# Rows transposed before their normalisation, and the multiplications that keep TensorE occupied at two starts

## The chip, the cores and the metric

The kernel runs on one core of a Trainium2 chip. The metric is the device time of one execution in microseconds (us). TensorE multiplies, VectorE, ScalarE and GpSimd do the elementwise work, and SyncE issues most of the DMAs. The rows of the profile call them PE (PEld is its weight load), DVE, ACT, POOL and SP.

## What is computed

Two layers of a decoder trunk for 512 prompt rows and 64 sample rows, 1024 wide, in f32. The change touches the first step of each layer, the normalisation and the input product, and the gating half `u` that comes out of it:

```python
def rmsnorm(x, g):
    y = x * rsqrt(mean(x * x, axis=-1) + EPS)
    return y * g

z = rmsnorm(x, g1) @ w_in                 # 1024 x 2560
a = gelu(z[..., :2 * D_A])                # u | va, 512 columns each
u, va = a[..., :D_A], rmsnorm(a[..., D_A:], av_g)
q, k = rmsnorm over heads of 64 columns;  vb = the last 512 columns
x = x + concat(u * chunk_mix(va), diff_attention(q, k, vb)) @ w_out
x = x + hierarchical_moe(rmsnorm(x, g2))  # 16 experts, two per row
```

The root `rsqrt(mean(x*x)+EPS)` is one number per row of x, so it can be multiplied onto x before the product or onto z after it.

## The kernel before

The rows stand in five tiles of 128 rows (`NT` = 5), four of the prompt and a fifth (`TP` = 4) with the 64 sample rows. One program holds every engine's instructions in an order that is written by hand; the engines meet in semaphores. `full[u]` says that PE has filled the PSUM bank `u`, `read[u]` that it has been read; `claim(u)` is PE's wait for the latter. The banks of this document are S0 and S1 (products of rows), T0 and T1 (transposes), J, I, O, and F (products of the gates). `keep_busy` multiplies the identity with itself into a bank that nobody reads.

**The input product.** For each tile ACT squares the row and sums it (`square_first`, L1150), POOL makes the root from the sum (`rsqrt`, L515 and L517), DVE multiplies x by the root into `hn` (`scaled`, L1387), PE transposes `hn` in two halves of four blocks (`turn_rows`, L671), and DVE multiplies the transpose by the gain g1 into `hT` (`turned`, L1393). PE then multiplies `hT` with the weights, which lie in a ring of six pieces of 1 MB; two pieces make 512 columns of w_in. The columns come in the order k, v, q, u, va. The transposes of tile t+1 are issued in the k columns of tile t, behind six of its eight steps (`rows`). ACT evacuates the products (`evacuate`) and squares those of k and q for the head norms.

**The gates.** `large("u", j)` computes u transposed, with the weights stationary, into the bank F; ACT applies Gelu from F into `catT`. u0 and u1 stand around the transposes of k, u2, u3 and the sample's `us` stand in the steps 0, 1 and 2 of the attention loop (`LARGE`). In a step n, PE does the scores of head n, transposes the probabilities of head n-2 (`turn_probs`), then the large product of the step and the small works of the sample (`ss` is the sample's scores, also in F), and multiplies the probabilities of head n-3 with v. DVE finds the maxima (`biggest`) and combines the two softmaxes (`combine`).

**The layer boundary.** The experts' results are scattered into `y_rows` by POOL and loaded back by ACT (`high_load`); DVE adds them to x (`add_high`, L1867), which releases `x_ready`. Then the chain of the input product begins again for layer 1. PE's own end of layer 0 is one multiplication of `flush`. SP issues the DMAs of the start in the order x tile 0, the identity (`id_in`), g1, weight pieces 0 and 1, x tiles 1 to 3 and the sample's, constants, pieces 2 to 5.

A matmul in f32 shows as two rows of the trace: eight steps of 128x512 are sixteen rows.

## Time and profile before

| | us |
|---|---|
| median of 3 runs | 1022.43 |
| lowest and highest | 1020.42, 1023.01 |
| the profiled execution | 1022.66 |
| its span, first to last instruction | 1020.8 |
| PE busy in it | 962.5 (94%) |
| mean granted clock of PE | 0.982 |

The span is the time from the first to the last instruction; the profiled execution is 1.86 us longer than it. PE is busy for 94% of the span, so an engine's work matters where PE waits for it. A granted clock of 1.00 is 2.4 GHz and one of 0.50 is 1.2 GHz.

### The profile page before, as it was taken

How to read it: one execution, taken by the hardware profiler on the slowest of the kernel's cores; microseconds unless marked ns; L12 is line 12 of the kernel's file. 1: busy time of each engine (PE TensorE's matmuls, PEld its weight loads, DVE VectorE, ACT ScalarE, POOL GpSimd, SP SyncE). 2: the span in 40 equal slices, each digit the busy share in tenths (PEclk: the TensorE clock that was granted, in tenths of full speed). 3: DMA queues.
4: the chain of work that ended last, by engine and by line, in shares of the span. 5: the costliest groups of instructions: out<-in, count | busy, mean ns of one | idle time of the engine just before them, and what ended most of it. 6: DMA issues, size and time to landing. Idle time of an engine off the chain costs nothing.

```text
span 1020.8 us, 13578 instructions
## 1 busy us (share of the span) xinstructions
PE 962.5 (94%) x4918; PEld 495.4 (49%) x4918; DVE 440.4 (43%) x1154; ACT 233.3 (23%) x483; POOL 191.5 (19%) x265
## 2 busy tenths in 40 slices
PE   6999999999998999999599999999989989999991
PEld 4444455556456444434254344655555554444340
DVE  2403122566346466551343111345563565555523
ACT  2101255542001011111121114555220011111110
POOL 2333201331101111111125031022220011111100
PEclk9999999999998999999899999999999999999996
DMA  8716003342511979998742150134252059799946
GB/s 335 267 31 257 1 1 129 103 146 91 220 42 63 383 259 370 420 421 328 240 144 83 49 209 1 68 109 160 63 208 103 21 222 367 274 381 412 403 153 209
DMA packets 39769, 197.72 MB, mean 194 GB/s; under 512 B 7632, under 2 KB 7760, under 8 KB 23824
## 3 DMA queue, kind: packets, MB, share of 16 engines
q1 hardware_dynamic: 19744, 136.22, 34.0%
q0 software_dynamic: 15888, 45.87, 12.8%
q10 hardware_dynamic: 4064, 14.68, 4.0%
q8 instruction: 42, 0.69, 0.3%
q14 instruction: 31, 0.25, 0.1%
HBM read 177.35 MB, written 29.88 MB: 203 GB/s over the span
## 4 chain that ended last, share of the span: by engine, by line
PE 84%; DVE 6%; DMA 4%; issue 2%; POOL 1%; ACT 1%; POOLq 0%; SPq 0%; ACTq 0%; DVEq 0%
PE ps L673 77%; PE ps L671 6%; DMA cat<-y_rows 1%; DMA x<-in_xp 1%; POOL st L517 1%; PE ps L688 1%; DMA y_rows<-hn,isca 1%; DVE cat L1720 1%; DVE hT L1393 0%; DMA hT<-h_rows,igat 0%; DVE tmp L1542 0%; DVE st L1543 0%; ACT hn L1306 0%; DVE st L1510 0%; DVE o_sb L1530 0%
## 5 line engine op out<-in xcount | busy, mean ns | idle before, releaser
L673 PE MATMUL ps<-ring,hT 128*128 128x512 f32 (+2 forms) x1056 | 382.4, 595 | 2.9 <-DVE hT L1393 2.5
L673 PEld LDWEIGHTS ps<-ring,hT 128*128 128x128 f32 (+2 forms) x1056 | 148.9, 166 | 198.1 <-issue 196.9
L673 PE MATMUL ps<-ring,cat 128*128 128x512 f32 (+2 forms) x560 | 195.4, 596 | 2.6 <-ACT hn L1306 2.4
L673 PEld LDWEIGHTS ps<-ring,cat 128*128 128x128 f32 (+2 forms) x560 | 72.9, 162 | 82.3 <-issue 79.4
L617 POOL DMA_INDIRECT y_rows<-hn,isca x28 | 28.1, 1003 | 250.1 <-ACT hn L1306 219.5
L673 PE MATMUL ps<-hT,ring 128*128 128x512 f32 (+1 forms) x256 | 71.8, 437 | 0.3 <-ACT cat L1194 0.3
L515 POOL TENSOR_SCALAR st<-st 128x1 f32<-128x1 f32 (+3 forms) x60 | 16.3, 272 | 282.2 <-ACT sqj L1150 106.4
L517 POOL TENSOR_TENSOR st<-st,half 128x1 f32<-128x1 f32 (+3 forms) x60 | 62.5, 1042 | 11.6 <-POOL st L515 11.1
L1861 DVE TENSOR_TENSOR hT<-ps,par 128x512 f32<-128x512 f32 x56 | 36.0, 685 | 56.0 <-PE ps L671 55.6
L1414 DVE TENSOR_REDUCE st<-sqj 128x8 f32<-128x512 f32 x20 | 13.5, 681 | 108.3 <-ACT sqj L1165 108.2
L1306 ACT COPY hn<-ps 128x1024 f32<-128x1024 f32 x28 | 28.4, 1013 | 118.3 <-PE ps L673 118.3
L673 PEld LDWEIGHTS ps<-hT,ring 128*128 128x128 f32 x256 | 38.1, 191 | 29.6 <-issue 28.4
L523 POOL DMA_DIRECT2D kc<-in_ck x32 | 25.3, 791 | 99.8 <-PE ps L673 78.8
L688 PE MATMUL ps<-c 128*128 128x128 f32 x164 | 27.4, 333 | 15.5 <-DVE x L1867 9.8
L1510 DVE TENSOR_REDUCE st<-ps 128x2 f32<-128x256 f32 (+3 forms) x32 | 26.3, 821 | 36.4 <-PE ps L673 36.3
L1231 ACT ACTIVATE ring<-ps,st 128x128 f32<-128x128 f32 (+3 forms) x64 | 33.2, 524 | 38.3 <-DVE st L1511 38.2
L610 POOL DMA_INDIRECT hT<-h_rows,igat x28 | 28.7, 1025 | 59.6 <-DVE isca L1759 30.3
L1165 ACT ACTIVATE sqj<-ps 128x512 f32<-128x512 f32 (+1 forms) x20 | 11.9, 596 | 119.1 <-PE ps L673 119.1
L1755 DVE TENSOR_REDUCE o_sb<-ps 128x4 f32<-128x12 f32 (+2 forms) x18 | 3.0, 167 | 83.5 <-PE ps L673 83.5
L1150 ACT ACTIVATE sqj<-x 128x1024 f32<-128x1024 f32 x10 | 10.6, 1058 | 121.1 <-DVE x L1576 100.6
L673 PE MATMUL ps<-vc,hT 128*128 128x512 f32 (+2 forms) x112 | 36.5, 598 | 0.8 <-issue 0.8
L523 POOL DMA_DIRECT2D vc<-in_cv x32 | 17.7, 552 | 91.4 <-PE ps L673 76.1
(249 smaller groups left out, 1172.7 us busy)
## 6 DMA issues: line engine op xcount, KB each, us to landing
ring<-in_w SPq DMA_DIRECT2D x82, 1024.0 KB
kc<-in_w SPq DMA_DIRECT2D x12, 1024.0 KB
vc<-in_w SPq DMA_DIRECT2D x10, 1024.0 KB
v<-in_w SPq DMA_DIRECT2D x10, 1024.0 KB
kva<-in_w SPq DMA_DIRECT2D x10, 1024.0 KB
kc<-in_ck POOLq DMA_DIRECT2D x32, 256.0 KB, 3.6
vc<-in_cv POOLq DMA_DIRECT2D x32, 256.0 KB, 3.2
h_rows<-qk ACTq DMA_DIRECT2D x10, 512.0 KB, 2.6
```

What stands on the lines that cost most here:

```text
L515: nc.gpsimd.tensor_scalar(stat["ms"][at, 0:n], src, 1.0 / size, EPS, ALU.mult, ALU.add).then_inc(*pool_c.inc())
L517: nc.gpsimd.tensor_tensor(dst, stat["ms"][at, 0:n], half[at, 0:n], ALU.pow).then_inc(*pool_c.inc(*label))
L523: pool.dma_start(buffer(b % 2, g), view(d[table][bass.DynSlice(l * NPOOL + page, 1)])).then_inc(*arrived[b % 2].inc("kv", b, by=16))
L610: pool.indirect_dma_start(hs[:, b, :], None, h_rows, bass.IndirectOffsetOnAxis(index, 0), bounds_check=TOK - 1, oob_is_err=False).then_inc ...
L617: pool.indirect_dma_start(rows, bass.IndirectOffsetOnAxis(index, 0), y_sb[:, b, :], None, bounds_check=rows.shape[0] - 1, oob_is_err=False ...
L671: ins = pe.transpose(out, lhsT, rhs)
L673: ins = pe.matmul(out, lhsT, rhs, start=start, stop=stop, skip_group_check=loose)
L688: pe.matmul(bank("J")[:, 0:P], ident, ident)
L1231: ins = nc.scalar.activation(e_sb[:, n % 2, m, 0:(i + 1) * P], bank(f"S{n % 2}", m)[:, 0:(i + 1) * P], ACT.Exp, bias=stat["nb"][:, c:c + 1 ...
L1306: nc.scalar.copy(y_sb[:, b, :], ps[:, 6:8, :].rearrange("p a n -> p (a n)")).then_inc(*read["O"].inc("down", *key))
L1510: link(vec.tensor_reduce(stat["mx"][:, c:c + 2], ps[:, b0:b0 + 2, 0:(i + 1) * P], AX.X, ALU.max))
L1861: vec.tensor_tensor(hsT[:, b, hf * HALF:(hf + 1) * HALF, :], bank(f"T{hf}").rearrange("p (j t) -> p j t", j=HALF), g, ALU.mult).then_inc(* ...
```

## The change

- **Transposes of x itself.** `scaled` is gone from the input product of both layers. PE transposes x as soon as the tile is there: in layer 0 when its load has landed, in layer 1 when `add_high` has released `x_ready`.
- **The root on the products.** ACT's evacuations of k, v, q and va multiply by the root of the row with the instruction's scale. u is transposed, so its roots must lie along the free axis: `root_diagonals` (DVE) multiplies the identity by each tile's roots, PE multiplies these by a matrix of ones behind the k columns (five matmuls into T0 and T1), and DVE copies the result into `roots`. `scale_gates` (DVE) multiplies each u product by them into `tmp`; Gelu (ACT) then reads `tmp`. The bank F is now released by DVE for u.
- **Places.** At the layer boundary DVE no longer waits two tiles behind `add_high`; `turned(t-1)` follows `add_high(t)` directly. One `memset` of hn is split, its second half stands in step 3 of the attention loop. ACT's Gelu of u0 and u1 moved behind the copies of kT and of qT.
- **Multiplications into nowhere.** At the start 18 multiplications of the 64-column tile `half` with itself, as soon as POOL has written it, in place of 12 with the identity when it has landed. At the boundary 30 of the identity into I right behind layer 0's last product, in place of 10 into J behind `x_ready`.

```diff
-            def keep_busy(n):
-                claim("J")
+            def keep_busy(n, u="J", operand=ident):
+                claim(u)
+                cols = operand.shape[-1]
                 for _ in range(n):
-                    pe.matmul(bank("J")[:, 0:P], ident, ident)
+                    pe.matmul(bank(u)[0:cols, 0:cols], operand, operand)
...
+            pe.wait_ge(*pool_c.at("half"))
+            keep_busy(18, operand=half[:, :])
             pe.wait_ge(id_in.sem, 16)
-            keep_busy(12)
             for l in layers():
                 if l:
-                    pe.wait_ge(x_ready.sem, l * NT + 1)
-                    keep_busy(10)
+                    keep_busy(30, "I")
+                def turn_input(t):
+                    if l == 0:
+                        pe.wait_ge(*dve_s.at("blank"))
+                        pe.wait_ge(x_in[t].sem, 16)
+                    turn_rows("h1", t, (x_ready.sem, l * NT + (t + 1)))
...
                 rows("k", 0)
+                pe.wait_ge(*dve_s.at("diagonals"))
+                for t in range(NT):
+                    u, n = ("T0", P) if t < TP else ("T1", NROW)
+                    if t in (0, TP):
+                        claim(u)
+                    mm(bank(u)[:, t % TP * P:t % TP * P + n], ones, diagonals[:, t * P:t * P + n], inc=full[u].inc("roots") if t >= TP - 1 else None)
                 rows("v", 1)
...
                         act.wait_ge(*full[u].at("z", name, t))
+                        act.wait_ge(*pool_c.at("rs1", t))
                         if name in "kq":
                             square_heads(name, t, u, slice(0, P))
-                        nc.scalar.copy(dst[:, t, :], bank(u)).then_inc(*read[u].inc("z", name, t))
+                        nc.scalar.mul(dst[:, t, :], bank(u), stat["rs"][:, t:t + 1]).then_inc(*read[u].inc("z", name, t))
...
                     if name == "u":
-                        nc.scalar.activation(catT[:, j, 0:TP * P], bank("F"), ACT.Gelu_apprx_tanh).then_inc(*read["F"].inc(name, j))
+                        act.wait_ge(*read["F"].at(name, j))
+                        nc.scalar.activation(catT[:, j, 0:TP * P], tmp[:, :], ACT.Gelu_apprx_tanh).then_inc(*act_s.inc(name, j))
...
+                def root_diagonals():
+                    vec.memset(ones, 1.0)
+                    for t in range(NT):
+                        dve.wait_ge(*pool_c.at("rs1", t))
+                        ins = vec.tensor_scalar(diagonals[:, t * P:(t + 1) * P], ident, stat["rs"][:, t:t + 1], None, ALU.mult)
+                    ins.then_inc(*dve_s.inc("diagonals"))
...
                     for t in range(NT):
                         if t == NT - 1:
                             sums("k", 0)
-                        scaled(t)
                         turned(t)
                     sums("k", 1)
+                    root_diagonals()
                     constants()
+                else:
+                    root_diagonals()
...
+                def scale_gates(name, j):
+                    dve.wait_ge(*full["F"].at(name, j))
...
+                    if before:
+                        dve.wait_ge(*act_s.at(*before))
+                    vec.tensor_tensor(out, src, by, ALU.mult).then_inc(*read["F"].inc(name, j))
+
+                for j in range(2):
+                    scale_gates("u", j)
                 dve.wait_ge(*read[HEADS_IN[TP]].at("qT", TP))
...
+                        elif name != "va":
+                            scale_gates(name, j)
+                    if n == 3:
+                        dve.wait_ge(*act_s.at("us", 0))
+                        link(vec.memset(hn[:, 1, :], 0.0))
...
-                for t in range(NT + 4):
-                    if 2 <= t < NT + 2:
-                        add_high(t - 2)
+                for t in range(NT + 1):
+                    if t < NT:
+                        add_high(t)
                     if l + 1 < L:
                         Count.layer = l + 1
-                        if 3 <= t < NT + 3:
-                            scaled(t - 3)
-                        if t == NT + 3:
+                        if t == NT:
                             sums("k", 0)
-                        if t >= 4:
-                            turned(t - 4)
-                        if t == NT + 3:
+                        if t >= 1:
+                            turned(t - 1)
+                        if t == NT:
                             sums("k", 1)
```

The lines moved with the edit: the changed kernel's L673 is L671 of before (transposes), L675 is L673 (products), L691 is L688 (`keep_busy`), L1412 is L1393 (`turned`) and L1918 is L1867 (`add_high`).

PE at the start of the program, before (x12 is twelve of them in a row; `c` holds the identity):

```order
L688 MATMUL ps<-c 128x128 x12
L671 MATMUL ps<-c,hn 128x128 x8
L673 MATMUL ps<-ring,hT 128x512 x6
L671 MATMUL ps<-c,hn 128x128 x8
L673 MATMUL ps<-ring,hT 128x512 x8
L671 MATMUL ps<-c,hn 128x128 x8
L673 MATMUL ps<-ring,hT 128x512 x8
L671 MATMUL ps<-c,hn 128x128 x8
L673 MATMUL ps<-ring,hT 128x512 x8
L671 MATMUL ps<-c,hn 128x128 x8
L673 MATMUL ps<-ring,hT 128x512 x34
L673 MATMUL ps<-ring,hT 64x512 x16
```

and of the changed kernel:

```order
L691 MATMUL ps<-half 64x64 x18
L673 MATMUL ps<-c,x 128x128 x8
L675 MATMUL ps<-ring,hT 128x512 x6
L673 MATMUL ps<-c,x 128x128 x8
L675 MATMUL ps<-ring,hT 128x512 x8
L673 MATMUL ps<-c,x 128x128 x8
L675 MATMUL ps<-ring,hT 128x512 x8
L673 MATMUL ps<-c,x 128x128 x8
L675 MATMUL ps<-ring,hT 128x512 x8
L673 MATMUL ps<-c,x 128x128 x8
L675 MATMUL ps<-ring,hT 128x512 x2
L675 MATMUL ps<-hn 128x128 x4
```

The small multiplications stand ahead of the transposes, these read x, and five matmuls of `hn` (the diagonals) stand between k and v.

PE at the boundary of the layers, before:

```order
L149 UNCONDITIONAL_BRANCH
L152 UNCONDITIONAL_BRANCH
L688 MATMUL ps<-c 128x128 x10
L671 MATMUL ps<-c,hn 128x128 x8
L673 MATMUL ps<-ring,hT 128x512 x6
L671 MATMUL ps<-c,hn 128x128 x8
L673 MATMUL ps<-ring,hT 128x512 x8
```

and of the changed kernel:

```order
L149 UNCONDITIONAL_BRANCH
L152 UNCONDITIONAL_BRANCH
L691 MATMUL ps<-c 128x128 x30
L673 MATMUL ps<-c,x 128x128 x8
L675 MATMUL ps<-ring,hT 128x512 x6
L673 MATMUL ps<-c,x 128x128 x8
L675 MATMUL ps<-ring,hT 128x512 x8
```

The 30 multiplications are in the place of the 10, but no longer behind the wait for `x_ready`, and the diagonals stand here too.

DVE at the boundary, before (L1867 is `add_high` where it reads `cat`, L1387 is `scaled`, L1393 is `turned`):

```order
L1867 SCALAR_TENSOR_TENSOR x<-cat,st,x 128x1024 x2
L1387 TENSOR_SCALAR hn<-x,st 128x1024
L1867 SCALAR_TENSOR_TENSOR x<-cat,st,x 128x1024
L1387 TENSOR_SCALAR hn<-x,st 128x1024
L1393 TENSOR_TENSOR hT<-ps,g_sb 128x4x128 x2
L1867 SCALAR_TENSOR_TENSOR x<-cat,st,x 128x1024
L1387 TENSOR_SCALAR hn<-x,st 128x1024
L1393 TENSOR_TENSOR hT<-ps,g_sb 128x4x128 x2
L1867 SCALAR_TENSOR_TENSOR x<-cat,st,x 64x1024
L1387 TENSOR_SCALAR hn<-x,st 128x1024
L1393 TENSOR_TENSOR hT<-ps,g_sb 128x4x128 x2
L1387 TENSOR_SCALAR hn<-x,st 128x1024
```

and of the changed kernel:

```order
L1918 SCALAR_TENSOR_TENSOR x<-cat,st,x 128x1024 x2
L1412 TENSOR_TENSOR hT<-ps,g_sb 128x4x128 x2
L1918 SCALAR_TENSOR_TENSOR x<-cat,st,x 128x1024
L1412 TENSOR_TENSOR hT<-ps,g_sb 128x4x128 x2
L1918 SCALAR_TENSOR_TENSOR x<-cat,st,x 128x1024
L1412 TENSOR_TENSOR hT<-ps,g_sb 128x4x128 x2
L1918 SCALAR_TENSOR_TENSOR x<-cat,st,x 64x1024
L1412 TENSOR_TENSOR hT<-ps,g_sb 128x4x128 x2
L1433 TENSOR_REDUCE st<-sqj 128x8
L1412 TENSOR_TENSOR hT<-ps,g_sb 128x4x128 x2
L1433 TENSOR_REDUCE st<-sqj 128x8
L1436 MEMSET hn 128x128
```

`turned` of tile 0 moved up from behind three `add_high` and two `scaled` to behind two `add_high`, and the matrix of ones with the diagonals stands at the end.

## Rows read from the trace of the kernel before

**Rows 1.** Section 4 of the page: shares of the chain that ended last.

```profile
PE 84%; DVE 6%; DMA 4%; issue 2%; POOL 1%; ACT 1%; POOLq 0%; SPq 0%; ACTq 0%; DVEq 0%
```

**Rows 2.** Timeline of the start: start us, us, engine, line, work [idle before <-releaser].

```profile
5.53 1.06 ACT L1150 ACTIVATE o_sb<-x 128x1024 f32<-128x1024 f32 x1 [3.07 <-DMA x<-in_xp]
...
5.73 4.39 PE L688 MATMUL ps<-c 128*128 128x128 f32 x24 [5.73 <-DMA c<-in_c]
...
9.24 0.75 DVE L1387 TENSOR_SCALAR hn<-x,st 128x1024 f32<-128x1024 f32 x1 [5.50 <-DMA g_sb<-in_g]
...
10.74 1.29 DVE L1393 TENSOR_TENSOR hT<-ps,g_sb 128x512 f32<-128x512 f32 x2 [0.75 <-PE ps L671]
...
12.29 5.39 PE L673 MATMUL ps<-ring,hT 128*128 128x512 f32 x12 [1.15 <-DVE hT L1393]
...
15.36 1.06 ACT L1150 ACTIVATE o_sb<-x 128x1024 f32<-128x1024 f32 x1 [8.68 <-DMA x<-in_xp]
...
18.65 1.09 PE L671 MATMUL ps<-c,hn 128*128 128x128 f32 x8 [0.98 <-DVE hn L1387]
```

**Rows 3.** Busy time by stretch of the start; (x) counts instructions.

```profile
core 0: us, PE busy (x) PEld busy (x) DVE busy (x) ACT busy (x) POOL busy (x), PEclk, DMA share, GB/s
7.00:8.00 1.00, 1.00 (x6) 1.00 (x6) 0.00 (x0) 0.00 (x0) 0.74 (x2) 1.00 0.90 318
9.00:10.00 1.00, 1.00 (x11) 0.93 (x9) 0.75 (x1) 0.00 (x0) 0.00 (x0) 1.00 1.04 426
10.00:14.00 4.00, 2.85 (x14) 1.72 (x13) 1.29 (x2) 0.00 (x0) 0.00 (x0) 1.00 1.00 417
```

**Rows 4.** Timeline of the boundary between the layers.

```profile
498.08 0.27 PE L671 MATMUL ps<-c 128*128 128x128 f32 x1
...
506.79 1.28 DVE L1867 SCALAR_TENSOR_TENSOR x<-cat,st,x 128x1024 f32<-128x1024 f32 x1 [6.99 <-DMA cat<-y_rows]
...
508.13 4.63 PE L688 MATMUL ps<-c 128*128 128x128 f32 x20 [9.78 <-DVE x L1867]
...
508.80 1.28 DVE L1867 SCALAR_TENSOR_TENSOR x<-cat,st,x 128x1024 f32<-128x1024 f32 x1 [0.73 <-DMA cat<-y_rows]
...
514.14 1.28 DVE L1393 TENSOR_TENSOR hT<-ps,g_sb 128x512 f32<-128x512 f32 x2
...
515.68 5.39 PE L673 MATMUL ps<-ring,hT 128*128 128x512 f32 x12 [1.39 <-DVE hT L1393]
```

**Rows 5.** Busy time and granted clock of two microseconds at the boundary.

```profile
503.00:504.00 1.00, 0.00 (x0) 0.00 (x0) 0.00 (x0) 0.00 (x0) 0.00 (x0) 0.87 0.00 0
513.00:514.00 1.00, 1.00 (x6) 1.00 (x6) 0.53 (x1) 0.97 (x2) 0.36 (x1) 0.51 0.85 269
```

**Rows 6.** The same ahead of the experts, in layer 0 and in layer 1.

```profile
315.00:316.00 1.00, 0.33 (x3) 0.33 (x4) 1.00 (x3) 0.41 (x2) 0.30 (x1) 1.00 0.88 360
316.00:317.00 1.00, 1.00 (x7) 1.00 (x6) 0.28 (x2) 0.10 (x1) 0.68 (x2) 0.50 0.41 164
817.00:818.00 1.00, 0.22 (x3) 0.16 (x2) 0.92 (x3) 0.58 (x2) 0.13 (x1) 1.00 0.72 291
```

**Rows 7.** Timeline of the end of the k columns of layer 0.

```profile
42.57 1.29 DVE L1393 TENSOR_TENSOR hT<-ps,g_sb 128x512 f32<-128x512 f32 x2 [5.20 <-PE ps L671]
...
43.78 0.68 DVE L1414 TENSOR_REDUCE st<-sqj 128x8 f32<-128x512 f32 x1
...
44.73 0.60 ACT L1165 ACTIVATE sqj<-ps 128x512 f32<-128x512 f32 x1 [6.67 <-PE ps L673]
...
46.89 0.48 DVE L1433 TENSOR_TENSOR tmp<-par 128x64 f32<-128x64 f32 x2
```

**Rows 8.** Timeline of the attention loop's steps 3 and 4, layer 0.

```profile
159.01 0.58 ACT L1247 ACTIVATE ring<-ps,st 128x384 f32<-128x384 f32 x1
...
159.25 0.33 PE L671 MATMUL ps<-c,ring 128*128 128x128 f32 x1
...
159.73 7.13 PE L673 MATMUL ps<-ring,hT 128*128 128x512 f32 x16 [0.15 <-ACT ring L1247]
```

More of the change, by code:

```diff
@@ L262, in program @@
                   v[:, 0:TP, :].rearrange("p t n -> p (t n)"), kva[:, 0:TP, :].rearrange("p t n -> p (t n)")]
+        diagonals = hn[:, 0, 0:NT * P]
+        roots, ones = hn[:, 1, 0:TOK], hn[:, 1, TOK:TOK + P]
         rows_of = sb("rows_of", [P, NT, E, 4], BF16)
@@ L502, in _ @@
         def _(pool):
-            nc.gpsimd.memset(half[:, :], -0.5).then_inc(*pool_c.inc())
+            nc.gpsimd.memset(half[:, :], -0.5).then_inc(*pool_c.inc("half"))
             pool.dma_start(pages[:, :], d["pages"]).then_inc(*pages_in.inc(by=16))
@@ L724, in rows @@
                             if t == 0:
-                                turn_rows("h1", 0, dve_s.at("hn1", 0))
+                                turn_input(0)
                             claim(u)
@@ L735, in rows @@
                             if c == 0 and k == KD - 3:
[L736 removed]
+                                turn_input(t + 1)
                 def sample_rows(name, low, high):
@@ L1164, in square_heads @@
                         act.wait_ge(*dve_s.at("ssk", NT - 1))
-                    nc.scalar.activation(sqj[at, t % 2, :], bank(u)[at, :], ACT.Square).then_inc(*act_s.inc("sq", name, t))
+                    nc.scalar.activation(sqj[at, t % 2, :], bank(u)[at, :], ACT.Square, scale=stat["rs"][at, t:t + 1]).then_inc(*act_s.inc("sq", name, t))
                 def evacuate(name, dst):
@@ L1185, in _ @@
                 square_heads("q", TP, "S0", LOW)
-                nc.scalar.copy(qz[LOW, TP, :], bank("S0")[LOW, :])
-                nc.scalar.activation(kva[HIGH, TP, :], bank("S0")[HIGH, :], ACT.Gelu_apprx_tanh).then_inc(*read["S0"].inc("z", "qva"))
+                nc.scalar.mul(qz[LOW, TP, :], bank("S0")[LOW, :], stat["rs"][LOW, TP:TP + 1])
+                nc.scalar.activation(kva[HIGH, TP, :], bank("S0")[HIGH, :], ACT.Gelu_apprx_tanh, scale=stat["rs"][HIGH, TP:TP + 1]).then_inc(*read["S0"].inc("z", "qva"))
                 act.wait_ge(*read["S0"].at("z", "qva"))
@@ L1202, in large @@
                         act.wait_ge(*dve_s.at("ssq", NT - 1))
-                    nc.scalar.activation(kva[:, j, :], bank("F"), ACT.Gelu_apprx_tanh).then_inc(*read["F"].inc(name, j))
+                    nc.scalar.activation(kva[:, j, :], bank("F"), ACT.Gelu_apprx_tanh, scale=stat["rs"][:, j:j + 1]).then_inc(*read["F"].inc(name, j))
                     act.wait_ge(*read["F"].at(name, j))
@@ L1434, in _ @@
                 vec.tensor_reduce(stat["lam"][:, 0:2], groups(tmp[:, 0:2 * DK], 2, DK), AX.X, ALU.add).then_inc(*dve_s.inc("lamdot"))
-                link(vec.memset(hn[:, :, :], 0.0))
+                dve.wait_ge(*full["T0"].at("roots"))
+                vec.tensor_copy(roots[:, 0:TP * P], bank("T0")).then_inc(*read["T0"].inc("roots"))
+                dve.wait_ge(*full["T1"].at("roots"))
+                vec.tensor_copy(roots[:, TP * P:TP * P + NROW], bank("T1")[:, 0:NROW]).then_inc(*read["T1"].inc("roots"))
+                link(vec.memset(hn[:, 0, :], 0.0))
                 for t in range(2, NT):
```

29 lines of the change are left out of this document (18 added, 11 removed).

## The prediction

> **What bounds the kernel now.** I read the page's chain of waits first: the reader is to see that PE holds 84% of it [rows 1], so a microsecond counts only where PE waits or does more. There are two places where PE waits for the input of a layer, and the change works on both; I then read their timelines, and last the places where the change puts new work beside PE.
>
> The start [rows 2]: x tile 0 has landed at 5.53, the identity at 5.73. PE multiplies the identity until DVE has made hn. DVE could not start that before 9.24, when g1 landed. The transposes are evacuated from 10.74, and 0.26 behind the end of that, at 12.29, PE starts its first product. It does 12 rows of it, then waits for the transposes of tile 1, which begin at 18.65: that tile landed at 15.36, and the square, root and multiplication took the 3.29 between. From 18.65 on the chain is PE without a gap.
>
> The boundary [rows 4]: PE's last row starts at 498.08 and ends at 498.35. It is idle until add_high of tile 0 is through at 508.07, and the first product starts at 515.68, again 0.26 behind the end of turned (514.14 + 1.28).
>
> The clock: at the boundary it fell from 2.4 to 1.2 GHz about 5.4 after PE's last row (granted 0.87 in the microsecond from 503), and rose 5.8 after PE had begun again (0.51 in that from 513) [rows 5]. At the start the record says 1.00 throughout, but the rows say otherwise: 6 of the 128x128 instructions in the microsecond from 7, 11 in that from 9 [rows 3].
>
> **The change, part by part,** against the profiled execution, 1022.66 (span 1020.8 and 1.86 around it, 0.23 above the median).
>
> *Start.* turned(0) needs g1 (9.24) and no longer hn: 9.24 + 1.29 + 0.26 = 10.79 is the earliest that PE can begin [rows 2]. The weights may be later. Tile 1, 0.52 MB, landed at 15.34 behind pieces 0 and 1 of 1.05 MB; at the 417 GB/s of 10 to 14 [rows 3] this puts piece 1 at 15.34 - 1.25 = 14.1 and piece 0 at 14.1 - 2.5 = 11.6, if they land in the order of issue; before, both were in time for 12.29. I take 11.3. The 12 rows last 12 x 0.43 = 5.15, so tile 1's transposes begin at 16.5 and not at 18.65: -2.2, between -2.7 (10.79) and -1.4 (12.0). The tile's landing (15.36) is hidden under that product. ACT's square and POOL's root are not removed, but they are now wanted only by the evacuation, 7 later.
>
> *Boundary.* DVE does add_high(0), add_high(1), turned(0). The second add waits for its data and ends at 508.80 + 1.28 = 510.08 [rows 4]; PE's transposes (508.1 to 509.8 even at 1.2 GHz) are ready by then. So turned ends at 510.08 + 1.28 = 511.36 and PE begins at 511.6 in place of 515.68: -4.0, between -4.1 and -3.5 if a semaphore or a later add comes between. Tile 1's transposes are wanted some 5 later and its add is done. Nothing else on DVE's or SP's queue is late: pieces 2 and 3 are wanted only at the v columns, 26 later.
>
> *Roots as a row.* PE does five more matmuls, ten rows, at 128 columns. In the fast microsecond eleven such rows start [rows 3], so this is 10 x 0.107 = 1.07 a layer. PE also waits for the diagonals. In layer 0 the k columns end at 44.73 (ACT's square of the last tile) and DVE's sum ends at 43.78 + 0.68 = 44.46 [rows 7]. Behind it now come a memset and five small multiplications. The nearest row is a 128x64 product, two in 0.48 [rows 7]: five at 0.15 to 0.3 and the memset 0.15 give 0.9 to 1.65; I take 1.15, near that row's 0.24 less the overlap that two without a wait between have. That ends at 45.6, plus a semaphore's 0.1: PE waits 1.0, between 0.7 and 1.5. Both ends move together with tile 4's transposes, so the start's gain does not cover it. Layer 1 has the same order. Sum: 2 x 2.07 = +4.1, between +3.5 and +5.1. Behind it, the copies of the roots and the split memset lie under v's 27 of PE.
>
> *Scaled evacuations.* A copy of 128x512 becomes an ACTIVATE; ACT's own, with a scale or without, take 0.60 [rows 7], there are 6.9 for each, and the roots are long there: nothing. If a root were late, PE would wait at the next claim of S0 or S1.
>
> *Gates through DVE.* The change adds a wait on DVE: in steps 0 to 2 scale_gates stands ahead of combine and biggest, so these, and ACT's exponentials behind them, wait for the product. PE spends these times in the next product (7.1), which hides them. What is visible is bank F: DVE needs 0.69 where ACT needed 0.60, three times 0.1 at most. In step 3 the chain us, Gelu, table, probabilities, sample's exponential (159.01) releases F for the first va product, for which PE waited 0.15 [rows 8]; with one more engine in it I add 0.4. The transposes of q gain 0.2, since ACT has no Gelu ahead of them. +0.3 a layer, together +0.6, between -0.4 and +1.2.
>
> Sum without the clock: -2.2 - 4.0 + 4.1 + 0.6 = -1.5, 1021.1 (between -3.9 and +1.3).
>
> *The clock.* The transposes now come early and the product late. At the start PE's small multiplications end near 5 (36 rows of half the columns, each half as long as a slow one of [rows 3], 3 to 4 in all, begun in the second microsecond), the transposes near 7, and the product starts at 11.3: some 4.5 idle. At the boundary 60 rows at 0.107 end at 504.9 if they start at once, at 506.5 if PE's branches take what they may; then idle to 508.1, 0.9 of transposes, and 2.6 idle until 511.6. Before, 5.4 of idling cost the clock [rows 5]. Ahead of the experts less was enough in layer 0: PE was a third busy in the microsecond from 315 and the clock read 0.50 from 316; in layer 1 a like stretch (0.22 busy from 817) kept it [rows 6]. So the new gaps are near the edge, and a second stretch of low activity in a row speaks for the fall. What a fall costs: the work done at half rate after the restart lasted 3 at the start (rows of 5.73 to about 8.8) and 5.8 at the boundary; half of it is lost, 1.5 to 2.9. I take 1.5 at the start and 2.3 at the boundary, where the fall may come late.
>
> The Trainium skill's page "TensorE: Matmul & The Clock Gate", section "What's actually happening", says that half rate is the default and activity releases it. By that rule alone the changed kernel pays at both places and ends at 1024.9; without a fall it ends at 1021.1. The rows at the boundary agree with the rule; those ahead of the experts show that the edge isn't sharp.
>
> **The rivals.**
> 1. *Both products start at 1.2 GHz* (forecast): -1.5 + 1.5 + 2.3 = +2.3, 1024.9. Chance 0.42.
> 2. *One of the two does*: -1.5 + 1.9 = +0.4, 1023.0. For it: layer 1 ahead of the experts kept its clock. 0.33.
> 3. *Neither*: 1021.1. The new multiplications carry the clock over. Against it are the 4.5 and the 2.6 of idling. 0.12.
> 4. *DVE becomes late in the attention loop*, the slower side. PE's transposes of head 2 stand at 159.25 [rows 8]; the combine ahead of them now starts behind the scaling of us, 156.2 + 0.4, and ends near 157.5. It decides from 1.8 of further lateness on (the memset of hn and the wait for Gelu stand right there); then F and the probabilities are late together, about 2 a layer: 1024.9 + 4 = 1028.9. 0.06.
> 5. *The start and the roots are better than priced*: piece 0 is there at 10.8, the diagonals cost 0.7 and both clocks hold: -3.9 or a little below, 1018.5. 0.07.
>
> That the change does not do what it says can only be at the start: if piece 0 lands at 12, the early transposes bring 1.4 and not 2.2; it is in the bounds.
>
> **How the numbers follow.** Beside these the half-rate stretch ahead of the experts may come or go with the shift, 1 to 1.5 either way. The range of eight in ten goes from a little below case 3, 1020.0, to 1028.0, which takes in case 1 with dear clocks (2.9 twice) and the roots at 5.1. About 0.3% (3.1) is what a measurement of this kernel can tell. Slower than 1025.5: four tenths of case 1, case 4, a little of 2: 0.27. Faster than 1019.4: case 5, a third of 3, some of 2: 0.16. The same: 0.57.
>
> **What would show it.** In the changed trace: the first 128x512 row near 11.3 and at 511.6; the distance of such rows, 0.43 at 2.4 GHz or 0.85 at 1.2 GHz, over the first dozen of each; a wait of PE of 1.0 for DVE ahead of ten rows that read hn, near 42 and 543; and the first va product, 0.4 later against the scores of step 3. The forecast is wrong if those rows stand 0.43 apart from the first, or if the wait for the diagonals is gone, because then the balance falls to the faster side.

## The result and the profile after

| | before | changed |
|---|---|---|
| median (22 runs each), us | 1020.5 | 1022.6 |
| lowest and highest | 1017.29, 1023.01 | 1020.95, 1025.15 |
| the profiled execution | 1022.66 | 1021.79 |
| its span | 1020.8 | 1020.1 |
| PE's last row ends | 998.74 | 999.74 |

The ratio is 1.0021 [1.0013, 1.0029]: the change costs 2.1 us. The forecast was +2.3 against the profiled execution, which gave 1024.9, and "the same" as the likeliest of faster, same and slower; the time lies inside the stated range, but the interval of the ratio leaves no room for "the same". The profiled execution of before lay 2.2 above the median of the 22 runs, and most of the difference between 1024.9 and 1022.6 comes from that.

The profiled executions alone say the opposite, 0.9 faster for the changed kernel. One pair can't be trusted at this size. At PE's end the changed kernel is 1.0 behind; then the chain goes through the last load of `y_rows` (start, duration, what), before:

```profile
1005.31 9.06 DMA cat<-y_rows
```

and in the changed kernel:

```profile
1006.34 7.48 DMA cat<-y_rows
```

No instruction of the change stands there. The page of the changed kernel, busy time, granted clock by slice and the chain:

```profile
PE 970.8 (95%) x4990; PEld 502.1 (49%) x4990; DVE 442.4 (43%) x1172; ACT 239.4 (23%) x485; POOL 191.4 (19%) x265
...
PEclk9999999999999999999989999999999999999996
...
PE 86%; DVE 6%; DMA 3%; issue 2%; ACT 1%; POOL 1%; SPq 0%; ACTq 0%; DVEq 0%; POOLq 0%
```

PE holds 86% of the chain where it held 84% [rows 1]: it waits less and does more.

**The start.** Timeline of the changed kernel, which answers to [rows 2]:

```profile
1.21 4.07 PE L691 MATMUL ps<-half 128*64 128x64 f32 x36 [1.21 <-POOL half L505]
...
5.66 1.51 PE L673 MATMUL ps<-c,x 128*128 128x128 f32 x8 [0.39 <-DMA c<-in_c]
...
7.76 1.29 DVE L1412 TENSOR_TENSOR hT<-ps,g_sb 128x512 f32<-128x512 f32 x2 [4.03 <-DMA g_sb<-in_g]
...
10.42 6.86 PE L675 MATMUL ps<-ring,hT 128*128 128x512 f32 x12 [3.25 <-DMA ring<-in_w]
...
12.26 0.34 PEld L675 LDWEIGHTS ps<-ring,hT 128*128 128x128 f32 x1 [0.52 <-issue]
13.11 0.33 PEld L675 LDWEIGHTS ps<-ring,hT 128*128 128x128 f32 x1 [0.52 <-issue]
...
14.04 1.06 ACT L1165 ACTIVATE o_sb<-x 128x1024 f32<-128x1024 f32 x1 [7.43 <-DMA x<-in_xp]
14.12 0.19 PEld L675 LDWEIGHTS ps<-ring,hT 128*128 128x128 f32 x1 [0.24 <-issue]
14.54 0.19 PEld L675 LDWEIGHTS ps<-ring,hT 128*128 128x128 f32 x1 [0.24 <-issue]
...
17.12 1.04 PE L673 MATMUL ps<-c,x 128*128 128x128 f32 x8
```

g1 landed at 7.76 and not at 9.24, the input was ready at 9.05, and PE then waited for weight piece 0 until 10.42. Twelve rows lasted 6.86 where they had lasted 5.39 [rows 2]: their weight loads stand 0.85 apart at 12.26 and 13.11, and 0.42 apart at 14.12 and 14.54. Tile 1 had landed by 14.04, well under the product. Tile 1's transposes begin at 17.12, 1.53 sooner than before; without the loss of 1.5 to the clock it would be 3.0.

**The boundary.** The same view of the boundary, which answers to [rows 4]:

```profile
497.78 0.27 PE L673 MATMUL ps<-c 128*128 128x128 f32 x1
...
499.36 6.94 PE L691 MATMUL ps<-c 128*128 128x128 f32 x60 [1.31 <-issue]
...
507.75 2.55 DVE L1918 SCALAR_TENSOR_TENSOR x<-cat,st,x 128x1024 f32<-128x1024 f32 x2 [8.30 <-DMA cat<-y_rows]
...
509.09 1.97 PE L673 MATMUL ps<-c,x 128*128 128x128 f32 x8 [2.80 <-DVE x L1918]
...
510.24 0.69 DVE L1412 TENSOR_TENSOR hT<-ps,g_sb 128x512 f32<-128x512 f32 x1
...
511.09 0.69 DVE L1412 TENSOR_TENSOR hT<-ps,g_sb 128x512 f32<-128x512 f32 x1 [0.16 <-PE ps L673]
...
512.05 6.93 PE L675 MATMUL ps<-ring,hT 128*128 128x512 f32 x12 [0.99 <-DVE hT L1412]
...
518.81 1.04 PE L673 MATMUL ps<-c,x 128*128 128x128 f32 x8
```

From the end of PE's last row (498.05; 498.35 before) to the first product it is now 14.00 and was 17.33: 3.33 less. The twelve rows last 6.93 and not 5.39, so tile 1's transposes are only 1.79 sooner by the same measure. add_high(0) could start 9.70 behind PE's last row and not 8.44 behind it as before [rows 4]; from its start to the product it is 4.30, and was 8.89.

The granted clock of the changed kernel at both places, in microseconds from 9, 10, 508 and 515 (columns as in [rows 3]):

```profile
9.00:10.00 1.00, 0.00 (x0) 0.00 (x0) 0.05 (x1) 0.00 (x0) 0.00 (x0) 0.99 1.00 418
10.00:11.00 1.00, 0.58 (x1) 0.50 (x2) 0.00 (x0) 0.00 (x0) 0.00 (x0) 0.50 1.03 434
...
508.00:509.00 1.00, 0.00 (x0) 0.00 (x0) 1.00 (x1) 0.00 (x0) 0.00 (x0) 0.66 0.99 401
515.00:516.00 1.00, 1.00 (x3) 0.46 (x3) 0.00 (x0) 0.00 (x0) 1.00 (x2) 0.92 0.77 172
```

At the start the record has 2.4 GHz until 10, in the idle time behind the transposes, and 1.2 GHz when the product begins. At the boundary it falls earlier, in the 2.8 of idling between the 30 multiplications and the transposes, so these run at half rate as well. Before, both products ran at 2.4 GHz (5.39 for twelve rows [rows 2, rows 4]), with the multiplications of the identity right ahead of the transposes; e4 and e6 put these back, one place each, and the product there takes 5.39 again.

**The roots.** The end of layer 0's k columns in the changed kernel, which answers to [rows 7]:

```profile
42.19 0.68 DVE L1433 TENSOR_REDUCE st<-sqj 128x8 f32<-128x512 f32 x1
42.84 0.17 DVE L1436 MEMSET hn<- 128x128 f32 x1
42.92 1.07 DVE L1439 TENSOR_SCALAR hn<-c,st 128x128 f32<-128x128 f32 x5
...
44.05 1.33 PE L675 MATMUL ps<-hn 128*128 128x128 f32 x10 [0.95 <-DVE hn L1439]
...
45.21 5.37 PE L675 MATMUL ps<-ring,hT 128*128 128x512 f32 x12
```

PE waits 0.95 for the diagonals (0.81 in layer 1) and spends 1.16 on ten rows.

**The gates.** The first va product of layer 0, which answers to [rows 8], starts its rows behind a wait of 0.41, where it was 0.15:

```profile
160.74 0.70 PE L675 MATMUL ps<-ring,hT 128*128 128x512 f32 x1 [0.41 <-ACT ring L1268]
```

Laid along PE's own path, the two profiles give this table. A stretch runs from one landmark to the next; the last row but one holds the router and the experts, which the change doesn't touch.

| stretch of PE (us) | before | changed | difference |
|---|---|---|---|
| start to tile 1's transposes | 18.65 | 17.12 | -1.53 |
| from there to u0, layer 0 and 1 | 95.14, 95.08 | 97.41, 97.28 | +2.27, +2.20 |
| u0 to the output product, layer 0 and 1 | 97.57, 97.55 | 97.81, 97.95 | +0.24, +0.40 |
| last row of layer 0 to tile 1's transposes of layer 1 | 22.55 | 20.76 | -1.79 |
| output product to the layer's last row, layer 0 and 1 | 286.99, 285.21 | 285.71, 285.70 | -1.28, +0.49 |
| behind PE's last row | 22.06 | 20.36 | -1.70 |

The change's own rows add up to -1.53 + 4.47 + 0.64 - 1.79 = +1.8, and the medians give +2.1. The two last rows are the noise in which these stand: the half-rate stretch ahead of the experts ran from 316.0 to 322.8 before [rows 6] and from 317.4 to 320.3 after, and in layer 1 there is one only in the changed kernel.

The first row holds such a chance too. In e10, whose start is that of the kernel before, tile 1 had landed by 14.05 and not 15.36, and its transposes began at 17.42 and not at 18.65. So 1.2 of the 1.53 come from a late load in one execution of before; against e10's start the sum would be +3.0, so that +1.8 and +2.1 lie so close is in part luck.

### The profile page after: what moved, and what is told of

It is laid out like the page before. It is cut to its first block, busy times and chain, and to the rows that moved or that the text cites. A ratio compares the mean times of both kernels' runs of the same rounds, so it can differ in the third digit from the quotient of the medians.

```text
span 1020.1 us, 13761 instructions
## 1 busy us (share of the span) xinstructions
PE 970.8 (95%) x4990; PEld 502.1 (49%) x4990; DVE 442.4 (43%) x1172; ACT 239.4 (23%) x485; POOL 191.4 (19%) x265
## 4 chain that ended last, share of the span: by engine, by line
PE 86%; DVE 6%; DMA 3%; issue 2%; ACT 1%; POOL 1%; SPq 0%; ACTq 0%; DVEq 0%; POOLq 0%
PE ps L675 78%; PE ps L673 7%; PE ps L691 1%; DMA cat<-y_rows 1%; POOL st L519 1%; DMA y_rows<-hn,isca 1%; DMA ring<-in_w 1%; DVE cat L1771 1%; DVE hT L1412 1%; DVE tmp L1588 0%; DVE st L1589 0%; ACT hn L1327 0%; DVE st L1556 0%; DVE o_sb L1576 0%; DVE tmp L1547 0%
## 5 line engine op out<-in xcount | busy, mean ns | idle before, releaser
L675 PE MATMUL ps<-ring,hT 128*128 128x512 f32 (+2 forms) x1056 | 385.8, 598 | 5.1 <-DMA ring<-in_w 3.2
L675 PEld LDWEIGHTS ps<-ring,hT 128*128 128x128 f32 (+2 forms) x1056 | 150.3, 168 | 201.0 <-issue 199.3
L675 PE MATMUL ps<-ring,cat 128*128 128x512 f32 (+2 forms) x560 | 195.4, 597 | 2.6 <-ACT hn L1327 2.4
L675 PEld LDWEIGHTS ps<-ring,cat 128*128 128x128 f32 (+2 forms) x560 | 73.0, 163 | 82.2 <-issue 79.3
L675 PE MATMUL ps<-hT,ring 128*128 128x512 f32 (+1 forms) x256 | 71.8, 438 | 0.5 <-DVE tmp L1498 0.5
L519 POOL TENSOR_TENSOR st<-st,half 128x1 f32<-128x1 f32 (+3 forms) x60 | 62.9, 1048 | 11.6 <-POOL st L517 11.4
L675 PEld LDWEIGHTS ps<-hT,ring 128*128 128x128 f32 x256 | 38.2, 191 | 29.9 <-issue 28.4
L1180 ACT ACTIVATE sqj<-ps,st 128x512 f32<-128x512 f32 (+1 forms) x20 | 13.7, 686 | 100.5 <-PE ps L675 94.0
L675 PE MATMUL ps<-vc,hT 128*128 128x512 f32 (+2 forms) x112 | 36.5, 598 | 0.8 <-issue 0.8
L1412 DVE TENSOR_TENSOR hT<-ps,g_sb 128x512 f32<-128x512 f32 x20 | 13.0, 687 | 54.5 <-PE ps L673 50.5
L1316 ACT ACTIVATE cat<-ps 128x256 f32<-128x256 f32 x28 | 10.7, 383 | 95.2 <-PE ps L675 95.2
```

The source lines that it names most:

```text
L519: nc.gpsimd.tensor_tensor(dst, stat["ms"][at, 0:n], half[at, 0:n], ALU.pow).then_inc(*pool_c.inc(*label))
L675: ins = pe.matmul(out, lhsT, rhs, start=start, stop=stop, skip_group_check=loose)
L1180: nc.scalar.activation(sqj[at, t % 2, :], bank(u)[at, :], ACT.Square, scale=stat["rs"][at, t:t + 1]).then_inc(*act_s.inc("sq", name, t))
L1412: vec.tensor_tensor(hT[:, hf * HALF:(hf + 1) * HALF, t * P:(t + 1) * P], bank(f"T{hf}").rearrange("p (j t) -> p j t", j=HALF), g, ALU.mult ...
```

## The experiments

Every ratio is to the kernel before, measured on the same chip beside it; the changed kernel stands at 1.0021. Each edit is on the changed kernel, except that of e10.

**e1: the gaps filled.** Multiplications of the identity behind tile 0's transposes too, and 42 in place of 30 at the boundary.

```diff
-                    keep_busy(30, "I")
+                    keep_busy(42, "I")
...
                             if t == 0:
                                 turn_input(0)
+                                keep_busy(8 if l else 14)
```

> The changed kernel with PE occupied in its gaps: 14 multiplications of the identity between the transposes of tile 0 and the first product of layer 0, 8 there in layer 1, and 42 in place of 30 at the boundary. Theory (the half-rate clock costs 1.7 at the start and 1.5 to 1.8 at the boundary): the granted clock stays at 1.00 over both, the first twelve rows of 128x512 take 5.2 in place of 6.9 at each, and the kernel is 3.3 faster than the changed one, about 1.3 faster than before (ratio 0.9987). Rival (the fillers themselves come late and push the product, or the weights and DVE bound it anyway): the first products begin 1 to 3 later and the time is within 0.5 of the changed kernel's 1.0021.

Measured: 1021.56, 1.0007 [0.9994, 1.0021]. Timeline of PE at the start and the boundary:

```profile
6.64 3.29 PE L691 MATMUL ps<-c 128*128 128x128 f32 x28
10.39 5.39 PE L675 MATMUL ps<-ring,hT 128*128 128x512 f32 x12 [0.47 <-DMA ring<-in_w]
...
497.69 9.62 PE L691 MATMUL ps<-c 128*128 128x128 f32 x84 [2.06 <-issue]
507.14 1.04 PE L673 MATMUL ps<-c,x 128*128 128x128 f32 x8
508.02 1.95 PE L691 MATMUL ps<-c 128*128 128x128 f32 x16
509.80 5.32 PE L675 MATMUL ps<-ring,hT 128*128 128x512 f32 x12
```

Both products run at full rate (5.39 and 5.32 for twelve rows), the boundary's transposes take 1.04 and not 1.97, and tile 1's transposes start at 15.62, 1.50 sooner than in the changed kernel. So the loss at the two products is the clock's, and the idle time ahead of them is what brings it. e1 fills both gaps of the boundary in one edit, the one ahead of the transposes and the one behind them. The other profiles show that the fall can come in either: with the boundary's program unchanged, the clock fell ahead of the transposes in the changed kernel and e8 (transposes 1.97), and behind them in e2, e3 and e6 (transposes 1.09, granted 0.50 or 0.62 in the microsecond from 512, 515 and 513). But the ratios show 1.4 and not 3 or more, and their intervals overlap. The profiled execution took 1018.28 at a mean granted clock of 0.992; the others lie between 0.985 and 0.990, and the six at 0.985 or 0.986 took 1021.6 to 1023.0. Something else loses the clock in them: e9 looks at that.

**e2: u left unscaled.** The five matmuls, the diagonals and the copies are gone and `roots` is filled with ones; u is left without its roots. This changes the values that reach the router, and the whole time (1049.85, 1.0284) can't be used: in its profile 50.62 lie behind PE's last row, where the changed kernel has 20.36. The stretch up to u0 can be used.

```diff
-                pe.wait_ge(*dve_s.at("diagonals"))
-                for t in range(NT):
...
-                    mm(bank(u)[:, t % TP * P:t % TP * P + n], ones, diagonals[:, t * P:t * P + n], inc=full[u].inc("roots") if t >= TP - 1 else None)
...
+                vec.memset(roots[:, 0:TP * P + NROW], 1.0)
```

> The changed kernel without the row of roots: no diagonals, no five matmuls and no wait for them; the gates are multiplied by ones, so u is left unscaled. It prices that part alone. Theory (0.9 to 1.0 of waiting and 1.1 to 1.2 of matmuls in each layer, all on the path): PE goes from the k to the v columns without a gap and the time is 4.1 less than the changed kernel's, ratio 0.998 against before. Rival (part of it is hidden or given back later, and the loss sits in the gates' way through DVE): 2 less or under, ratio 1.000.

Measured, from tile 1's transposes to u0: 95.08 in both layers, where the changed kernel has 97.41 and 97.28. The row of roots costs 2.33 + 2.20 = 4.5. In PE's timeline k runs into v in one group:

```profile
41.28 19.05 PE L675 MATMUL ps<-ring,hT 128*128 128x512 f32 x44
```

**e3: the roots one tile later.** The same five matmuls, behind the first tile of the v columns in place of behind k.

```diff
-                pe.wait_ge(*dve_s.at("diagonals"))
-                for t in range(NT):
...
+                            if (c, t, k) == (1, 0, KD - 1):
+                                row_of_roots()
```

> The changed kernel with the five matmuls of the roots behind the first tile of the v columns, 6.9 later. Theory (of the 2.1 a layer 0.9 is the wait for DVE's diagonals): that wait is gone, the matmuls' 1.1 stays, 1.8 less than the changed kernel in all, ratio 1.0004. Rival (the wait moves to another place, since DVE's copies of the roots and the sums behind them are now later): no gain, ratio 1.002.

Measured: 1020.5, 1.0006 [0.9991, 1.0021]; from tile 1's transposes to u0 96.20 in both layers, which is 1.2 and 1.1 less than in the changed kernel and 1.1 more than without roots. The ratio's interval overlaps that of the changed kernel, so the step is shown by the stretch, not by the whole time. PE's timeline has no wait at them:

```profile
45.80 6.17 PE L675 MATMUL ps<-ring,hT 128*128 128x512 f32 x14
51.81 1.22 PE L675 MATMUL ps<-hn 128*128 128x128 f32 x10
```

Of the 2.2 a layer one half is the wait, which is only a matter of place; the other half is the ten rows themselves.

**e4: the old boundary.** 10 multiplications into J behind `x_ready`, all else as changed.

```diff
-                    keep_busy(30, "I")
+                    pe.wait_ge(x_ready.sem, l * NT + 1)
+                    keep_busy(10)
```

> The changed kernel with the boundary's multiplications as before: ten of the identity behind x_ready, into bank J, everything else as changed. Theory: the transposes of tile 0 now end about 4.7 behind x_ready at half rate, so the product begins about 2.5 later than in the changed kernel, but with the clock risen or about to rise it gets 1 to 1.5 back: 1 to 1.5 slower than the changed kernel (ratio 1.0033). Rival (what counts at the boundary is that the clock has risen when the product begins, not when the product begins): equal to or faster than the changed kernel, ratio 1.002 or less.

Measured: 1023.39, 1.0042 [1.0029, 1.0055]. The profile of e4:

```profile
508.17 4.64 PE L691 MATMUL ps<-c 128*128 128x128 f32 x20 [10.16 <-DVE x L1919]
512.60 1.09 PE L673 MATMUL ps<-c,x 128*128 128x128 f32 x8
515.00 5.39 PE L675 MATMUL ps<-ring,hT 128*128 128x512 f32 x12 [1.31 <-DVE hT L1413]
```

With transposes of x but twenty slow rows ahead of them, the product starts 16.99 behind the last row (498.01), against 14.00 in the changed kernel and 17.33 before: nearly the whole gain of the boundary comes from the moved multiplications, since the transposes were waiting for them and not for `scaled`. The product then runs at full rate, so the net of the move is 1.5 in the profile (tile 1's transposes 22.2 behind the last row, 20.8 in the changed kernel), and 0.21% by the ratios.

**e6: the old start.** 12 multiplications of the identity once it has landed.

```diff
-            pe.wait_ge(*pool_c.at("half"))
-            keep_busy(18, operand=half[:, :])
             pe.wait_ge(id_in.sem, 16)
+            keep_busy(12)
```

> The changed kernel with the start's multiplications as before: twelve of the identity, when it has landed, ahead of the transposes. Theory (the early start of the product gains what the half-rate clock then takes back): PE is occupied until 10 or 11, the transposes come then, the first product at 12.2 with a clock that rises at once or is at 2.4 GHz, tile 1's transposes at 17.4 to 18.5; the changed kernel had 17.12, so the time is 0 to 1 more than its, ratio 1.002 to 1.003. Rival (the small tile's multiplications carry the early start's gain of 1.8): ratio 1.0039 or more.

Measured: 1024.3, 1.0034 [1.0019, 1.005]. The product of e6 starts at 13.49 and tile 1's transposes at 18.72, as late as in the kernel before (18.65): x is there sooner, but the multiplications of the identity hold the transposes until 11.01. They took 5.49 here and 4.39 before [rows 2]. So at the start too it is the small tile that frees the transposes: 1.6 in the profile. But 1.1 of this is the longer multiplications of this one execution; with the 4.39 of before it would be about 0.5. By the ratios it is 0.13%, with intervals that overlap, so the size of this gain is not shown. The spread is wide, from 1018.47 (mean clock 0.992) to 1027.15 (0.981).

**e8: turned(t) right behind add_high(t).** DVE no longer does the second add ahead of the first turned.

```diff
-                for t in range(NT + 1):
-                    if t < NT:
-                        add_high(t)
+                for t in range(NT):
+                    add_high(t)
...
-                        if t >= 1:
-                            turned(t - 1)
+                        turned(t)
```

> The changed kernel with one move: at the boundary DVE does turned of each tile right behind its add_high, so the transposes of tile 0 do not wait for add_high of tile 1. Theory (DVE's order holds the product there, not the data): the first product of layer 1 begins 1.0 earlier, behind x_ready by 2.3 to 3.0 in place of 3.0 to 3.6; ratio 1.001. Rival (the transposes at half rate bound it, 1.7 behind x_ready, and the fall of the clock takes the rest): 0 to 0.4, ratio 1.002.

Measured: 1022.07, 1.002 [1.001, 1.0031]: no gain. The profile of e8 shows DVE waiting for PE in place of the data:

```profile
508.81 1.97 PE L673 MATMUL ps<-c,x 128*128 128x128 f32 x8 [2.36 <-DVE x L1918]
...
509.96 0.69 DVE L1412 TENSOR_TENSOR hT<-ps,g_sb 128x512 f32<-128x512 f32 x1 [1.21 <-PE ps L673]
...
511.77 7.21 PE L675 MATMUL ps<-ring,hT 128*128 128x512 f32 x12 [0.99 <-DVE hT L1412]
```

From the transposes' start to the product it is 2.96, exactly as in the changed kernel (509.09 to 512.05). While the transposes run at half rate they, and not DVE's order, bound the chain.

**e7: e1, e3 and e8 together,** with 5 multiplications in place of 8 behind layer 1's transposes.

> The changed kernel with three repairs: the gaps at both starts filled with multiplications (14 and 5 behind tile 0's transposes, 42 in place of 30 at the boundary), the row of roots behind the first tile of the v columns, and turned of tile 0 ahead of add_high of tile 1 at the boundary. Theory (prices from the runs so far: clock 3.3, wait for the diagonals 1.8, add_high(1) 1.0): 6.1 less than the changed kernel, ratio 0.996 against before. Rival (the prices don't add up, because the clock falls ahead of the experts and the loads of the weights decide again): ratio 0.999 to 1.000.

Measured: 1017.1, 0.9978 [0.9966, 0.9989], 0.43% better than the changed kernel, a little less than the 0.6% that was expected. The product of the boundary starts 13.76 behind PE's last row (495.22 to 508.98) and at full rate; in the changed kernel it is 14.00 and half rate.

**e9: e7 with the router filled too.** What is left in e7 is a fall ahead of the experts. 4 multiplications stand ahead of PE's wait for the last output product and 3 behind the last transposes there, in both layers.

```diff
+                keep_busy(4)
                 pe.wait_ge(*read["S1"].at("y", 1, TP - 1))
...
                 turn_half("x", TP - 1, 1)
+                keep_busy(3)
                 logits(TP - 1, (1,))
```

> The three repairs and seven more multiplications of the identity ahead of the experts of each layer (four while DVE adds the last output rows, three while it evacuates the last transposes), where the clock of before fell in layer 0 and not in layer 1. Theory (the falls there, not only at the two starts, make single executions differ by 1 to 2 each): the granted clock reads 1.00 there in both layers, the mean of the clock is 0.991 to 0.992 in every execution and the time 1 to 2 less than with the three repairs alone, ratio 0.995. Rival (the fillers are late for what PE has to do there): equal to the three repairs or 0.5 slower.

Measured: 1016.11, 0.9962 [0.9948, 0.9975]. The granted clock ahead of the experts, e7:

```profile
315.00:316.00 1.00, 1.00 (x6) 1.00 (x7) 0.77 (x4) 0.92 (x1) 0.04 (x1) 0.50 0.00 0
818.00:819.00 1.00, 1.00 (x7) 0.94 (x7) 0.00 (x0) 0.00 (x0) 0.00 (x0) 0.50 0.02 8
```

and e9, where it read 1.00 in each of these microseconds:

```profile
315.00:316.00 1.00, 1.00 (x11) 1.00 (x10) 0.72 (x4) 0.66 (x1) 0.30 (x1) 1.00 0.00 0
818.00:819.00 1.00, 1.00 (x12) 0.91 (x9) 0.76 (x5) 0.00 (x0) 0.45 (x1) 1.00 0.00 0
```

The mean clock of e9's five executions is 0.990 to 0.992, e7's eleven have 0.984 to 0.989. The medians differ by 1.0 and the intervals overlap, so the size of this step is less sure than its mechanism; the spread, 1.2 us over five runs in place of 4.5 over eleven, fits. By the ratios it is 0.59%, 6 us, better than the changed kernel, and it is the best version here together with e11: it beats both kernels.

**e10: the kernel before, filled.** The rival to all this is that the clock alone is worth the gain and the transposes of x nothing. 36 multiplications behind layer 0's last row, 14 behind `x_ready`, 10 behind tile 0's transposes of layer 1, and the router's.

```diff
                     pe.wait_ge(x_ready.sem, l * NT + 1)
-                    keep_busy(10)
+                    keep_busy(14)
...
                                 turn_rows("h1", 0, dve_s.at("hn1", 0))
+                                if l:
+                                    keep_busy(10)
```

> The kernel before with multiplications alone added: 36 of the identity right behind layer 0's last product and 14 in place of 10 behind x_ready, 10 behind the transposes of tile 0 of layer 1, and the seven ahead of the experts of each layer. No transposes of x, no roots behind the products. Theory (ahead of the experts a held clock is worth 1 to 2; at the boundary the kernel before gains nothing from it, because its chain of root, multiplication and DVE's order sets the product): ratio 0.998 to 0.999, granted clock 0.991 in every execution. Rival (the clock alone makes the best kernel so far, and the transposes of x are worth nothing): ratio 0.9965 or less.

Measured: 1019.46, 0.9993 [0.9981, 1.0005], at clocks of 0.989 to 0.992. Holding the clock is worth little to the kernel before, whose products were fast already: its interval includes 1, where a gain of 0.1 to 0.2% was expected. Against e9, with the clock held in both, the change's own terms read cleanly: tile 1's transposes 17.42 and 15.78 (-1.64), last row to product at the boundary 17.95 and 13.74 (-4.21), tile 1's transposes to u0 95.08 and 96.19 (+1.11 in each of the layers). That is -3.6, and with the gates' +0.6 it is -3.0; the ratios differ by 0.31%, 3.2 us. A part of the 4.21, about 1.4, is e10's second add_high, which waited 2.10 for its data and 0.73 before [rows 4].

**e11: shorter fills.** e9 with 35 in place of 42 at the boundary, since 42 end at 506.5 and x was ready at about 504.6, and 12 for 14 at the start.

> The three repairs and the multiplications ahead of the experts, with fewer of them at the two starts: 35 in place of 42 at the boundary, where PE was still at them 1.6 behind x_ready, and 12 in place of 14 in layer 0. Theory (those 1.6 are on the path and the clock holds over the shorter fill): the first product of layer 1 begins about 1.5 earlier against PE's last row of layer 0, 1.3 to 1.6 less in all, ratio 0.9948. Rival (the shorter fill lets the clock fall in some executions): the median as before, 0.996, with a wider spread.

Measured: 1015.71, 0.9961 [0.9948, 0.9975]: the same as e9. Last row (494.70) to product (507.62) is 12.9 in place of 13.7, so the shorter fill brings its 0.8 there. It was expected to bring 1.5 in all, and the ratios show 0.1. The mean clocks are lower than e9's (0.988 to 0.991), and in the profiled execution the stretch from the output product to PE's end in layer 1 is 286.74 where e9 has 285.24. The trace has the place of these 1.5: granted 1.00 over both starts, and then in e11

```profile
739.00:740.00 1.00, 1.00 (x7) 1.00 (x7) 0.86 (x3) 0.00 (x0) 0.07 (x1) 0.50 0.00 0
```

That is 230 us behind the boundary, close behind a wait of PE's of 1.74 for ACT, which the other profiles have there too. e10, with the longer fills, lost its clock at the same point (0.50 from 743), e2 and e3 did at the same point of layer 0, and e9 kept it. So in this execution the shorter fill held the clock where it stands, and a fall at a third place, which no kernel here fills, gave the gain back. Whether shorter fills make falls likelier was the rival; five runs don't settle it.

## Why the forecast came out as it did

| term (us) | forecast | measured |
|---|---|---|
| start, without the clock | -2.2 (-2.7 to -1.4) | -3.0 (-1.8 against e10) |
| boundary, without the clock | -4.0 (-4.1 to -3.5) | -3.3 |
| roots, both layers | +4.1 (+3.5 to +5.1) | +4.5 |
| gates, both layers | +0.6 (-0.4 to +1.2) | +0.6 |
| sum without the clock | -1.5 | -1.2 |
| clock, start | +1.5 | +1.5 |
| clock, boundary | +2.3 | +1.5 |
| sum | +2.3 | +1.8 (medians +2.1) |

The mechanism is the forecast's first case: both products start at 1.2 GHz, and that turns a small gain into a small loss. e1 shows that it is the clock, e2 and e3 that the roots cost about what they were priced at. That the sum came within 0.5 is partly luck: the start came out 0.8 better, and the boundary 0.7 worse with a clock 0.8 cheaper. The start's 0.8 is itself a late load of the one profiled execution before: e1's tile 1 transposes come at 15.62, 1.8 ahead of e10's.

**The step that failed is the last one, from the sum to "the same".** The text took about 0.3% (3.1) as what a measurement can tell, so its own +2.3 counted as no change, and "the same" got 0.57 and slower 0.27. Here 22 runs of each give 1.0021 [1.0013, 1.0029], which is 0.08% to either side: +0.21% is within the stated 0.3% and yet is clearly slower. The chances for a sign should have come from the cases. The likeliest, +2.3, is slower, and by the prediction's own chances cases 1 and 4 together make slower 0.48.

**The second failed step is the first line of the sum, the base.** It was made against one profiled execution at 1022.66, said to stand 0.23 above the median; that was the median of three runs, and the median of 22 is 1020.5, 2.2 below the profiled execution. Every time in the prediction carries these 2.2 us, and a forecast of +2.3 on a base 2.2 too high reads as 1024.9 where 1022.6 was measured. The profiled execution had a half-rate stretch of 6.8 us ahead of the experts and a last load of 9.06 that came out shorter elsewhere; how much of the 2.2 is theirs is not known. Over all the profiles but e2's the last load took between 6.3 and 9.1. With three runs up to 2.6 apart, the base was known to one or two us at best, and the range should have said so.

**Start.** The earliest product was put at 10.79 by g1's landing at 9.24. In the changed kernel's trace g1 was there at 7.76 and the bound was piece 0, at 10.42; over the experiments piece 0 was there between 10.3 and 11.2 (11.19 in e3). The landing of an 8 KB load in one execution is no bound. Piece 0 at 11.6, by the order of landing and the rate of 417 GB/s, was 1.2 too late, and the 11.3 that was taken 0.9. The first twelve rows were priced right.

**Boundary.** It was 0.7 dearer than said, a little outside the bounds. The chain that was counted held: two adds back to back (507.75 + 2.55 = 510.30), then turned, 511.78, then 0.27 to the product. From add_high(0)'s start that is 4.30, and 4.8 was said, since the second add had no wait. What was taken as fixed is the other part: y_rows was there 9.70 behind PE's last row and not 8.44. Over the experiments this runs from 8.3 (e10) to 9.7 without any pattern in the edits, so it is an unknown of its own with 1.3 to either side, and the bounds had nothing for it. The transposes at half rate hid behind the second add but for 0.16; e8 shows that they bound the chain if that add is gone. Of the 30 multiplications the later case came true: they ended at 506.3.

**Clock at the boundary.** 5.8 at half rate was taken from the restart before; the stretch here was from 508.3 to 515.2, of which the product saw 3.1, so the loss is half of that. At the start the product saw 3.0 in the same way. Both fit "what is done at half rate lasts twice as long"; for this execution the length was taken too long. But it isn't fixed. From the product's first row to tile 1's transposes it is 5.23 at full rate (e1). With the clock down it is 6.7 to 6.9 at the start in the changed kernel, e2, e4 and e8 and 7.93 in e3; at the boundary it is 6.8 to 7.1 in the changed kernel, e2, e3 and e8 and 8.03 in e6. So a fall cost 1.5 to 1.8 in most of these profiles and 2.7 to 2.8 in two, and the forecast's 2.3 lies between.

The Trainium skill's page "TensorE: Matmul & The Clock Gate", section "What's actually happening", has half rate as the default and full rate as what activity releases. By that rule alone the changed kernel paid at both products, and the trace agrees at both (granted 0.50 in the microsecond from 10 and in that from 512).

**DVE in the attention loop** (case 4) didn't become late: the wait at the first va product went from 0.15 to 0.41, 0.3 and not 0.4. The scaled evacuations stayed off the path, as said, though each is a little dearer: 0.69 and 0.68 in the changed kernel, where the square took 0.60 [rows 7] and the copy behind it 0.58.

## What to carry to other kernels

When a change makes an input ready earlier but not the work that it feeds, look at what TensorE does in between: multiplications of nothing belong right ahead of the expensive product, behind the small transposes, and not only in the idle time before these; both gaps brought a fall here. Filled so, with the places ahead of the experts filled too, the roots one tile later and turned ahead of the second add, the change is worth 0.3% over a filled kernel of before; unfilled it costs 0.2%. And price a change of a few microseconds against a median of many runs, with the chance stretches of the profiled execution (a half-rate stretch elsewhere, a late last load) read out first.

## What was not expected of the hardware

- The granted clock reads 1.00 at the start, while the rows show half rate: e9's eight transposes from 5.69 lasted 1.66 and the changed kernel's 1.51, where e1's lasted 1.09. Durations have to be trusted before the record there.
- At the boundary the multiplications start 1.31 behind PE's last row with 30 of them, and 2.06 to 2.34 behind it with 35 or 42 (e1, e7, e9, e11), though no wait is shown. e6, with 30, has 1.57, and e10, with 36 in the kernel before, 1.52. What this depends on stays open; it was not tried apart.
- Ahead of the experts the clock fell in layer 0 alone in the kernel before and in both layers in the changed one, at nearly the same work. From the fastest run to the slowest it is 8.7 us in e6 and 6.9 in e3, and 1.2 in e9, which fills that place (twelve, twelve and five runs). The filled kernels keep a higher mean clock, 0.990 to 0.992 in e9 against 0.982 to 0.986 in the changed one.
- Loads of one size land at different times: g1 (8 KB) at 7.8 or 9.2, tile 1 by 14.05 or 15.36 in two kernels with the same start, weight piece 0 between 10.3 and 11.2, the first y_rows between 8.3 and 9.7 behind PE's last row, the last one after 6.3 to 9.1. Each of these is as large as a term of the sum.
